# Attention probabilities and the first layer norm's rows turned through DRAM instead of on TensorE

## The reference, cut to what matters

```python
h = _layernorm(x, ln_emb_g, ln_emb_b)
proj = h @ w_in[l]                    # 13376 columns, split into all branches

def attend(qblk):                     # 8 MLA heads over 256 keys
    s = jnp.einsum('bqhd,bkhd->bhqk', qblk, k).astype(jnp.float32) * scale
    p = jax.nn.softmax(s, axis=-1).astype(v.dtype)
    return jnp.einsum('bhqk,bkhd->bqhd', p, v)

s = jnp.einsum('bqhd,bmhd->bhqm', q, k).astype(jnp.float32) * (MEM_HD ** -0.5)
p = jax.nn.softmax(s, axis=-1).astype(v.dtype)    # 4 memory heads over 256 memory tokens
return jnp.einsum('bhqm,bmhd->bqhd', p, v).reshape(B, S, MEM_WIDTH)
```

## Time and profile before

| | |
|---|---|
| median of three runs | 1715.19 us (1714.43 to 1719.62) |
| the profiled execution's own time | 1715.36 us |
| its span | 1713.6 us, so 1.76 us lie around the span |
| PE busy | 1706.1 us, 100% of the span |
| DVE, ACT, POOL busy | 1157.7, 812.5 and 94.7 us |
| data moved | 391.69 MB, 229 GB/s over the span |

### The profile page before, as it was taken

One profiled execution on the slowest core, in us unless ns is written; L12 is line 12 of the kernel. 1 busy time (PEld: TensorE's weight loads), 2 busy tenths in 40 slices (PEclk: granted clock), 3 DMA queues, 4 the chain that ended last, 5 costly groups with the idle time before them and its releaser, 6 DMA issues.

```text
span 1713.6 us, 20425 instructions
## 1 busy us (share of the span) xinstructions
PE 1706.1 (100%) x8742; PEld 1416.2 (83%) x8742; DVE 1157.7 (68%) x996; ACT 812.5 (47%) x669; POOL 94.7 (6%) x87
## 2 busy tenths in 40 slices
PE   9999999999999999999999999999999999999999
PEld 8888888888878788888888888888888888888886
DVE  4764556677675746444666679888879798655445
ACT  4454555455444535444444526554555545443332
POOL 0000002213021300000000000000000000000000
PEclk9999999999999999999999999999999999999999
DMA  9666875555455567646888958778787876878553
GB/s 364 239 248 214 257 236 202 173 187 171 163 177 178 173 197 260 243 172 221 270 268 261 381 172 266 240 248 251 231 260 238 245 243 164 267 244 307 196 197 123
DMA packets 140250, 391.69 MB, mean 229 GB/s; under 512 B 9088, under 2 KB 60672, under 8 KB 125696
## 3 DMA queue, kind: packets, MB, share of 16 engines
q1 hardware_dynamic: 132448, 370.86, 64.5%
q0 software_dynamic: 2720, 10.49, 3.4%
q10 hardware_dynamic: 4992, 9.05, 1.4%
HBM read 361.91 MB, written 27.79 MB: 227 GB/s over the span
## 4 chain that ended last, share of the span: by engine, by line
PE 98%; DVE 1%; DMA 0%; issue 0%; ACT 0%; POOL 0%; DVEq 0%; POOLq 0%
PE pair L2089 21%; PE pair L2091 21%; PE pair L2090 21%; PE pair L2363 4%; PE pair L2364 4%; PE pair L2365 4%; PE pair L2063 3%; PE side L2343 3%; PE side L2344 3%; PE side L2345 3%; PE pair L2061 1%; PE pair L2343 1%; PE pair L2345 1%; PE pair L2344 1%; PE pair L2073 1%; PE side L2171 1%
## 5 line engine op out<-in xcount | busy, mean ns | idle before, releaser
L1348 DVE TENSOR_TENSOR weight_lo<-raw,weight_hi 128x2048 fp32r<-128x2048 f32 x210 | 482.1, 2298 | 417.8 <-ACT weight_hi L940 416.4
L940 ACT ACTIVATE weight_hi<-raw 128x2048 fp32r<-128x2048 f32 x210 | 402.4, 1916 | 535.5 <-DMA raw<-in_stream 535.2
L2089 PE MATMUL pair<-weight_hi,act_both 128*128 128x512 f32 x928 | 369.3, 398 | 0.6 <-DVE weight_lo L1348 0.6
L2091 PE MATMUL pair<-weight_hi,act_both 128*128 128x512 f32 x928 | 361.7, 390 | 0.0
L2090 PE MATMUL pair<-weight_lo,act_both 128*128 128x512 f32 x928 | 361.4, 389 | 0.0
L2089 PEld LDWEIGHTS pair<-weight_hi,act_both 128*128 128x128 f32 x928 | 174.2, 188 | 36.9 <-issue 1.3
L2091 PEld LDWEIGHTS pair<-weight_hi,act_both 128*128 128x128 f32 x928 | 174.2, 188 | 36.6
L2090 PEld LDWEIGHTS pair<-weight_lo,act_both 128*128 128x128 f32 x928 | 174.4, 188 | 35.6 <-issue 0.2
L1247 ACT ACTIVATE part_hi<-part_raw 128x2048 fp32r<-128x2048 f32 x60 | 113.8, 1912 | 117.0 <-DVE part_raw L1831 48.5
L1811 DVE TENSOR_TENSOR part_lo<-part_raw,part_hi 128x2048 fp32r<-128x2048 f32 x60 | 136.6, 2283 | 38.6 <-ACT part_hi L1247 38.6
L2089 PE MATMUL pair<-weight_hi,ff_both 128*128 128x512 f32 x352 | 136.9, 389 | 0.0
(11 more groups left out here) (316 smaller groups left out, 2545.1 us busy)
## 6 DMA issues: line engine op xcount, KB each, us to landing
raw<-in_stream SPq DMA_DIRECT2D x256, 1024.0 KB, 5.4
part_raw<-in_stream SPq DMA_DIRECT2D x30, 1024.0 KB, 7.0
part_raw<-in_stream POOLq DMA_DIRECT2D x10, 1024.0 KB, 10.3
scratch<-spill ACTq DMA_DIRECT2D x32, 256.0 KB, 5.1
ln_rows<-in_ln_rows SPq DMA_DIRECT2D x6, 1024.0 KB, 8.0
gate<-scratch SPq DMA_DIRECT2D x12, 512.0 KB, 6.7
ff_scratch<-ff_blocks SPq DMA_DIRECT2D x11, 512.0 KB, 5.3
ff_land<-ff_scratch SPq DMA_DIRECT2D x44, 128.0 KB, 5.3
```

Of the source, the lines that this page charges most:

```text
L940: act.activation(hi_of(n), raw_of(n), ACT.Copy).then_inc(extra_h if extra(n) else h_ready, 1)
L1348: dve.tensor_tensor(lo_of(n), raw_of(n), hi_of(n).bitcast(F32), ALU.subtract)\
L2089: pe.matmul(out, hi[:, k0 + k, tok], w_hi[:, k, :], start=first and k == 0, stop=False)
L2091: mm = pe.matmul(out, lo[:, k0 + k, tok], w_hi[:, k, :], start=False, stop=last and k == 3)
```

## The change

It takes two jobs away from PE: the 32 transposes of the first layer norm and the 48 of the attention probabilities. Both now go the way of `squares`, `save` and `fetch`.

- *Layer norm.* Statistics and normalisation begin one slot sooner (5 and 7 instead of 6 and 8). DVE transposes squares into four buffers `ln_blocks` in slots 10, 11, 11 and 12. GpSimd, not SP, issues the DMAs: four saves and sixteen fetches on its own queue. ACT and DVE split the four landed columns in slots 15, 16, 16 and 17, and PE waits for one column before each of the four `c_q` pieces 16 to 19 instead of for all of them before piece 16.
- *Attention.* DVE transposes the squares right behind its division in slot s+2. SP saves them behind the load of piece s+6 and fetches them with four DMAs behind the load of piece s+7 (`carry_prob`); ACT makes `prob_t` from what landed in slot s+6, PE multiplies behind piece s+6 and the split is in slot s+7. The squares of a unit are 64 floats wide, 256 bytes per row of a fetch.
- *Recurrence.* A pair of heads takes 12 slots instead of 13; the memory heads' units move four slots sooner, to 110, 113, 116 and 119.
- *Layout.* All scratch tensors that hold squares are kept by token tile (`by_tile`), so a save writes 2 KB runs instead of 512 bytes; fetches still read 512 bytes. `qg_blocks` has one buffer instead of two. The warm-up's 20 matmuls go to four banks instead of one; some semaphores are merged.

```diff
-STATS_SLOT, NORM_SLOT = 6, 8
+STATS_SLOT, NORM_SLOT = 5, 7
-LN_SLOT = 11
-HG_SLOT, HG_STEPS, PAIRS = FIRST["i_hg"] + 1, 13, 4
+LN_BLOCKED = (10, 11, 11, 12)
+LN_SPLIT = (15, 16, 16, 17)
+HG_SLOT, HG_STEPS, PAIRS = FIRST["i_hg"] + 1, 12, 4
...
+            def carry_prob(n):
+                u = unit_at(n, 6)
+                if u is not None:
+                    sp.wait_ge(p_blocked, u + 1)
+                    sp.dma_start(prob_scratch[u].rearrange("t p e -> p t e"),
+                                 prob_blocks[:].rearrange("p (t e) -> p t e", t=TT)).then_inc(p_out, 16)
+                u = unit_at(n, 7)
+                if u is not None:
+                    sp.wait_ge(p_out, 16 * (u + 1))
+                    if u:
+                        sp.wait_ge(pt_done, u)
+                    for m in range(QUADS):
+                        src = of_square(prob_scratch[u], m)
+                        sp.dma_start(prob_land[SQ * m:SQ * m + SQ].rearrange("p (s e) -> p s e", e=2 * SQ), src)\
+                            .then_inc(p_in, 16)
...
-                sp.dma_start(turned_scratch[u].rearrange("m p e -> p m e"), blocks).then_inc(done, 16)
+                sp.dma_start(turned_scratch[u].rearrange("t p e -> p t e"), by_tile(blocks)).then_inc(done, 16)
...
+            def save_ln(c):
+                pool.wait_ge(rows_blocked, c + 1)
+                pool.dma_start(ln_scratch[c].rearrange("t p e -> p t e"), by_tile(ln_blocks[c][:])).then_inc(ln_out[c % 2], 16)
+            def fetch_ln(c):
+                pool.wait_ge(ln_out[c % 2], 16 * (c // 2 + 1))
+                if c >= 2:
+                    pool.wait_ge(ln_in[c % 2], 16 * QUADS)
+                for m in range(QUADS):
+                    src = of_square(ln_scratch[c], m)
+                    pool.dma_start(ln_land[SQ * m:SQ * m + SQ, c].rearrange("p (s e) -> p s e", e=P), src)                        .then_inc(ln_in[c % 2], 16)
+            save_ln(0)
+            save_ln(1)
+            fetch_ln(0)
+            save_ln(2)
+            fetch_ln(1)
+            save_ln(3)
+            fetch_ln(2)
+            fetch_ln(3)
...
+                for c in range(4):
+                    if n == LN_SPLIT[c]:
+                        act.wait_ge(ln_in[c % 2], 16 * QUADS * (c // 2 + 1))
+                        act.activation(squared(act_hi[:, 4 * c:4 * c + 4, :]), slices(ln_land[:, c]), ACT.Copy)\
+                           .then_inc(turned_h, 1)
...
-                u = unit_at(n, 3)
+                u = unit_at(n, 6)
                 if u is not None:
-                    act.wait_ge(p_turned, u + 1)
+                    act.wait_ge(p_in, 16 * QUADS * (u + 1))
...
-                    last.then_inc(p_done, 1)
+                    chain(last)
+                    if u:
+                        dve.wait_ge(p_out, 16 * u)
+                    for t in range(TT):
+                        dst = prob_blocks[:].rearrange("p (t m k b) -> p t k m b", m=QUADS, t=TT, k=2)[:, t]
+                        last = dve.transpose(dst, prob[:, t, :].rearrange("p (k m b) -> p k m b", k=2, m=QUADS))
+                    last.then_inc(p_blocked, 1)
...
+                for c in range(4):
+                    if n == LN_BLOCKED[c]:
+                        dve.wait_ge(h_done, 4 + c + 1)
+                        for t in range(TT):
+                            squares(ln_blocks[c][:], t, h_tok[:, t, c * 512:(c + 1) * 512], rows_blocked)
+                    if n == LN_SPLIT[c]:
+                        dve.wait_ge(turned_h, c + 1)
...
-                    pe.wait_ge(p_done, u + 1)
+                    pe.wait_ge(pt_done, u + 1)
-                    for k in range(2):
-                        for t in range(TT):
-                            at_ = k * T + t * P
-                            mm = pe.transpose(side[3][:, at_:at_ + P], prob[:, t, k * P:(k + 1) * P], ident[:])
-                    mm.then_inc(p_turned, 1)
-                if LN_SLOT <= n < LN_SLOT + 4:
-                    for b in (2 * (n - LN_SLOT), 2 * (n - LN_SLOT) + 1):
-                        turn(b, h_tok, 0, h_done)
...
-            pe.wait_ge(turned_l, 8)
-            t_phase("c_q", 4, 4, act_hi, act_lo)
+            for j in range(4):
+                n = FIRST["c_q"] + j
+                pe.wait_ge(turned_l, j + 1)
+                t_piece(Nth(n), GROUP["c_q"], j, 4, act_hi, act_lo)
+                after(n)
```

More of the change, by code:

```diff
@@ L331, in encoder_program @@
         root_ready = sem("root_ready")
+        ln_out = [sem(f"ln_out{i}") for i in range(2)]
+        ln_in = [sem(f"ln_in{i}") for i in range(2)]
         h_done = sem("h_done")
@@ L429, in encoder_program, with by_tile, of_square @@
         block = ctx.enter_context(nc.Block())
+        def by_tile(blocks):
+            return blocks.rearrange("p (t m) e -> p t (m e)", t=TT)
+        def of_square(rows, m):
+            return rows.rearrange("t (i a) (m e) -> m a (t i) e", i=QUADS, m=QUADS)[m]
         def slices(land):
@@ L633, in save_rows @@
             def save_rows(i):
-                sp.wait_ge(rows_blocked, 2 + i + 1)
+                sp.wait_ge(rows_blocked, 6 + i + 1)
                 sp.wait_ge(rows_out, 16 * (2 + i))
-                save(2 + i, f_blocks[:] if i < F_ROWS else qg_blocks[:, i % 2], rows_out)
+                save(2 + i, f_blocks[:] if i < F_ROWS else qg_blocks[:], rows_out)
             def fetch_f(i):
@@ L671, in _ @@
                 load(Nth(HG_END + 10 + k))
-            load(Nth(HG_END + 12))
+                carry_prob(HG_END + 10 + k)
+            loads(HG_END + 12, HG_END + 13)
             first = FIRST["branch"]
@@ L1605, in slot @@
                     wait_taken(dve, GROUP[name] + c)
[L1606 to L1615 removed]
+                    rows, blocks = (f_rows, f_blocks[:]) if i < F_ROWS else (qg_rows, qg_blocks[:])
+                    if i:
+                        dve.wait_ge(rows_out, 16 * (2 + i))
                     for t in range(TT):
@@ L2140, in four_blocks, with turn @@
                 mm.then_inc(piece_used, 1)
-            def turn(b, src, k0, rows):
+            def turn(b):
                 t, k = b // 4, 4 * (b % 4)
-                if b == 0 and not k0:
-                    pe.wait_ge(ident_in, 16)
-                pe.wait_ge(rows, k0 + b + 1)
+                pe.wait_ge(h_done, 8 + b + 1)
                 if b >= 4:
-                    pe.wait_ge(turned_l, k0 + b - 3)
+                    pe.wait_ge(turned_l, 4 + b - 3)
                 for j in range(4):
-                    mm = pe.transpose(turn_bank(b)[:, j * P:(j + 1) * P], src[:, t, (k + j) * P:(k + j + 1) * P],
+                    mm = pe.transpose(turn_bank(b)[:, j * P:(j + 1) * P], z[:, t, (k + j) * P:(k + j + 1) * P],
                                       ident[:])
@@ L2314, in turn_first_tile @@
                 if q:
-                    turn(q - 1, z, 8, h_done)
+                    turn(q - 1)
             begin_group(GROUP["w_o"] + 3)
@@ L2329, in _ @@
                     if (t, q) in turn_after:
-                        turn(turn_after[t, q], z, 8, h_done)
+                        turn(turn_after[t, q])
             for j in range(4, 8):
```

153 lines of the change are left out of this document (72 added, 81 removed).

## The result

The changed kernel takes 1729.67 us (median of 5 runs, 1725.59 to 1732.44) beside 1716.48 for the kernel before (five runs now; the three of the table above had 1715.19): ratio 1.0076, 95% interval [1.0065, 1.0088], 13 us slower. The profiled execution has a span of 1727.9 us, 14.3 more than before.

What follows compares the result with a forecast made beforehand. PE's own instruction stream, busy 1706.1 of 1713.6 us, was taken as the bound. From 1715.4, less 3.5 and 6.1 for transposes and 2.0 for a wait, plus 3.6 lost on late rows, gave 1707.4 us; range 1703.0 to 1718.4.

Steps and rivals of the forecast that it cites:

- part 3: Layer norm rows through GpSimd's queue: 20 DMAs at 1.21 us, landings 7.0 and 5.5; PE waits before `c_q`, 3.6 us lost.
- The bounds: Layer norm rows on GpSimd's queue: quicker landings (5.1, 3.1) give 1703.8 us, slower ones (median 10.3) give 1718.4.
- The quick bound: GpSimd's queue with landings of 5.1 (save) and 3.1 (fetch): column 2 at 104.5, wait 0.4 or none, 1703.8 us.
- the bullets: Issue and landing times listed for GpSimd's four saves and four column fetches, from 79.4 to the last landing at 113.4.
- Part 1: Transposes leave PE: 3.5 us saved in the layer norm, 6.1 us for the attention probabilities.
- the prediction's sign against it: PE's busy time falling much less than 9.6 us would mean transposes were partly hidden and the chain was misread.
- ACT's copy at about half of 1.05: Attention probabilities: ACT's copy counted in a 16 to 18 us path, against 21.8 available; costed at nothing.
- Part 2: Attention: PE's 2.0 us wait for DVE's probabilities, behind a pair's reciprocal, goes away; 2.0 us saved.
- R1: Rival: GpSimd's queue is slow, landings of 10.0 to 11.4 us; PE waits 14.6, total 1718.4 us; chance 0.15.
- R2: Rival: DVE locks GpSimd out, its DMAs take 2.5 us instead of 1.21; PE waits 21.7, total 1725.5; chance 0.10.
- R3: Rival: attention gives it back, waits for DVE return at three reciprocals, 8.1 us lost, total 1715.5; chance 0.13.

Runs made afterwards that it cites:

- the probe: The changed kernel with 36 more GpSimd DMAs near 610 us, three groups of twelve (128 KB, 64 KB, 512 KB), no waits within a group: 1725.88 us.

## Why the prediction was wrong

I forecast 1707.4, a range from 1703.0 to 1718.4, and measured 1729.67. The step that failed is in part 3, "GpSimd then issues 20 DMAs in order", which made the sum's term of 3.6 us lost out of what measured 21.8. I took the queue to be held by the DMAs' own time, 1.21 us each, and by the saves that it waits for. Their own time was about half of that, 0.58 to 0.88, and the landings that I took, 7.0 and 5.5, were right at the medians (6.7 and 5.6). What was missing is that the queue takes only so many runs at a time: 32.1 us of stops, and a last column at 132.5 instead of 113.4. The rows before could not show it. The ten DMAs of the earlier trace rows are of another form (1 MB each, added into their target by `accum_op`) and come one by one over 365 us, so none ever found another in its way; I read a price per transfer off them and used it for twenty in a burst. The bounds shared the fault: both took other landings and left the queue endless. (The quick bound's 104.5 for column 2 counts 1.2 us too much; by the bullets it is 103.3, and the bound, without a wait, stays 1703.8.)

- **Part 1** held for the layer norm: 3.5 predicted, 3.6 measured at piece 15. That PE's busy time fell by far less than 9.6, the prediction's sign against it, came for the larger part of the slower clock. For the probabilities, with the rows on PE, the end of the span moved by 5.5. Of the 6.1 + 2.0 that I summed, 1.6 went to the new wait for `prob_t`, 0.6 was lost by piece 64, and 0.4 I did not trace. My words "ACT's copy at about half of 1.05" gave the copy no queue; a sigmoid of 3.2 us stood before it in the one slot where pair and unit end together.
- **Part 2**: the 2.0 us wait is gone, and no other took its place on DVE.
- **Part 3, what was late next**: I had the bounds and angles behind column 2 set the end. In the change they set nothing; the last column landed at 132.5, after they had finished at 130.1. In the kernel with all on SP, the places in the order did count, by another route than I had: a late weight load ahead of a column on ACT and DVE.
- **The clock** was in no term of mine. With it 15.6 us of waiting cost 21.8, some 5.6 of them in slower products. I priced every wait as if PE went on at full speed behind it.
- **R1** (slow landings) fell: 2.5 to 8.0 us. **R2** came out near the time (1725.5) for a wrong reason: no DMA took over 0.9 us, and the longest stop ran on beside an idle DVE. The port lock of the Trainium skill ("SBUF — State Buffer", SBUF: two separate sides) is thus not what held this queue. The Trainium skill's page "DMA: Bandwidth & Descriptors", section SWDGE vs HWDGE vs iDMA, has what would fit: GpSimd writes the descriptors of its DMAs into rings in SBUF. That the queue stops because these rings are full is my reading of the probe; no run here shows the rings, and the section does not say how many transfers they hold. **R3** fell: no wait for DVE came back at the reciprocals, and the 1.6 us above are ACT's.

## What to carry to other kernels

A duration per DMA is not a rate of DMAs: before a burst is put on a queue, look in the trace for a burst on that queue, and where there is none, bound the burst by one landing per transfer. Twenty DMAs at 5.6 us each would have been 112 us, and would have said that the question is open. In this kernel the fetches in short runs belonged on SP's queue and four saves did no harm on GpSimd's; turning the norm's rows on PE was as good as either. And a wait of PE can cost more than its length, here 1.4 times.

## What was not expected of the hardware

- GpSimd's queue: in the probe DMAs of 256 runs went out three at a time, of 128 KB or of 512 KB alike, and those of 128 runs seven at once, apart from the first of the second and third batch, which went alone; DMAs of 512 runs went one at a time.
- TensorE's clock was at its 1.2 GHz level behind an idle stretch of 3.2 us, and in the windows of the change it is granted 0.79, 0.64 and 0.72 in a row.
- Beside other traffic, weight loads on SP's queue took long. In the kernel with all on SP it was 10.0 us beside the rows (issued at 96.65) and 14.1 right behind the 2 MB of `h_scratch` (108.49), against 4.6 to 5.1 for the loads from 65.62 to 76.50. The rows are not needed for it: the kernel before has 9.7 us for the load at 107.25, behind the same stores. The kernels with the rows through DRAM also have one wait of 1.2 to 1.4 us for `rope_x` near 345 to 365 us, of which at most 0.5 is left with the rows on PE. ACT comes to it late there, behind a weight load that landed in 6.1 to 6.3 us instead of 4.8; what delayed that load stays open.
